# Ahead of a head loop: the rotary key is spread by GpSimd, two value tiles are evacuated by VectorE, and a chunk's rests are made later

## The chip, the cores and the metric

The kernel runs on 1 core of a Trainium2 chip. Times are microseconds on the device for one execution of the whole program. A core has TensorE (PE in the profile), VectorE (DVE), ScalarE (ACT), GpSimd (POOL) and SyncE (SP, which here only issues DMA transfers). Each works off its own list of instructions in order, and they wait for each other by semaphores.

## The reference, cut to what matters

Two blocks are computed on 256 tokens of width 1024 in float32. The change touches the second block, which puts 16 learned tokens ahead (so L = 272) and runs two kinds of causal attention side by side on the same normed input.

```python
u = rmsnorm_2(h, pre_norm_g[l])
proj = u @ w_in[l]
(cq, ckv, k_pe_raw, z_mla, fq, fk, fv, f_logit, z_fox, gate_a, gate_b) = jnp.split(proj, split_idx, axis=-1)
q = (rmsnorm_2(cq, mla_q_norm_g[l]) @ w_uq[l])      # 16 heads, 64 plain + 32 rotary columns
kv = (rmsnorm_2(ckv, mla_kv_norm_g[l]) @ w_ukv[l])  # 16 heads, 64 key + 64 value columns
k_pe = rope_2(k_pe_raw, pos)[:, None]               # one rotary key, the same for all heads
k_m = jnp.concatenate([k_nope, jnp.broadcast_to(k_pe, (B, MLA_HEADS, L, MLA_ROPE_DIM))], axis=-1)
o_mla = causal_block_attention(q_m, k_m, v_mla, MLA_SCALE)
o_fox = causal_block_attention(fox_heads(fq), fox_heads(fk), fox_heads(fv), FOX_SCALE, cum)
```

Here `k_m` is the keys of the latent attention (each head: its own 64 rows, and the rotary key that all share), `v_mla` its values, and `fq`, `fk`, `fv` belong to the attention with forget gates.

## The kernel before

Every float32 product is three matmuls of rounded halves, x_hi·w_hi + x_lo·w_hi + x_hi·w_lo (lines 472 to 474). So each operand must be split: ScalarE writes the rounded part (w_hi, s_hi, g_hi), and VectorE then writes the **rest**, value minus rounded part (w_lo, s_lo, g_lo). The large weights come in 56 chunks of 2 MB, each as two halves g = 0, 1 in `w_raw`. SyncE loads half g of chunk c once the rest of the same half of chunk c-1 is made (semaphore `w_lo_ok`). Small weights come in units (`w_side` into `s_raw`).

TensorE's order is written out by hand. Its results go to two accumulator banks `acc` in turn, as numbered by `acc_plan()`. Before tile n is begun, tile n-2 must have been evacuated (`acc_free`). Other results have banks of their own.

The stretch at issue lies ahead of the last loop, which runs over 32 heads (16 latent, 16 with forget gates). TensorE does there, in this order:

- `fk` 0 to 3: key tiles of the forget attention, from chunk `C_FK`. VectorE scales them (`keys_scaled`, line 2301). The tiles from `fk` 4 on need chunk `C_FK + 1`, in the loop.
- Transposes of the normed latents `cqn` in tiles 0, 1 and then 2 (`cqkv_turn`). ScalarE and VectorE split them into g_hi and g_lo. The transpose of tile 2 waits until the rest of tile 0 is made.
- `uk` 0 to 7: the latent keys, two heads each. ScalarE evacuates the even ones (1597, 1598), VectorE the odd ones (2335, 2336).
- `uv`: six value tiles of 512 columns, for the meta tokens (t = 2), then t = 0, then t = 1. Key `("uv", i, cc)` counts i in this order. ScalarE evacuates all six (`carry`, line 1240).
- `uq` 0 to 2: queries of heads 0 to 2. VectorE evacuates them (`query`, line 2361). They need the split unit `U_Q` (ScalarE 1226, then `rest_side` on VectorE, line 1743), and `uq` 2 goes into the bank of `uq` 0.
- Scores of heads 0 and 1 (line 1033), and the loop, which begins with the first half of what rides along with it: tile `fk` 4.

The shared rotary key stands in bank 6. ScalarE copies it into the keys `kT` of all 16 heads, four heads to an instruction (line 1587). `rest_half(c, slot, g)` makes half g of the rests of chunk c, 128x2048 (line 1830). GpSimd clears two tiles for the meta values (lines 450, 452), and issues eight small DMA transfers that place the meta rows `vu_rows` in them (line 458) once ScalarE has written these (`vu_ok`). VectorE waits for their landing (`um_landed`) in the loop, since `vu_rows` lies where `fk` 4 is to be written.

Of the kernel before, what the change touches and what calls it, by code (L numbers as in the profile page):

```python
# [23 lines left out]
ACT = mybir.ActivationFunctionType  # L24
AX = mybir.AxisListType.X

P = 128
R = 2
S = P * R
M = 16  # L30
L = M + S
D = 1024
KT = D // P
CH = 512
# [6 lines left out]
NH = 16  # L41
# [79 lines left out]
USE = acc_plan()  # L121
# [42 lines left out]
def two_blocks(nc, w_main, w_side, params, rows, c_l0, c_l1, c_b2, ident_d, x_d, x_t, meta_d, pos_d, out_d):  # L164
    ctx = ExitStack()
    with ctx:
# [3 lines left out]
        def sem(name):  # L170
            return ctx.enter_context(nc.semaphore(name))
# [27 lines left out]
        def ar(off, *shape):  # L199
            n = int(np.prod(shape))  # L200
            v = arena[:, off:off + n]
            names = "abcd"[:len(shape)]
            if len(shape) == 1:
                return v
            return v.rearrange(f"p ({' '.join(names)}) -> p {' '.join(names)}", **dict(zip(names[1:], shape[1:])))
# [46 lines left out]
        o_fox, y_mix = ar(7296, R, D), ar(9344, R, D)  # L252
        q_h, sm, pt = ar(14720, 2, S), ar(15232, 2, 416), ar(16064, 640)
        meta_p = [ar(off, R, GROUP * M) for off in (5760, 6016, 14720, 14976)]
        vu_rows, vf_rows = ar(1088, D)[0:M, :], [ar(4736, CH)[32 * c:32 * c + M, :] for c in range(2)]
        meta_v = [v_mm[:, 0:CH], v_mm[:, CH:D], f_vm[:, 0:CH], f_vm[:, CH:D]]
        root_p = stat[:, 8:24].rearrange("p (r a) -> p r a", r=R)
        b2c, b2k = ar(16704, L + S), ar(15232, L + P)
# [7 lines left out]
        hm, um, m_tmp = ar(11904, D), ar(12928, D), ar(3328, KT, M)  # L266
        sq = ar(9840, D)
        gain_u, scale_u, half_u, fin_u = pcol("norm_mix0", 0, KT), small[:, 32:34], small[:, 34:36], small[:, 36:38]
        kp, f_row = ar(2560, L), ar(2832, 4, L)
        last_gh, last_gl, last_sh, last_sl = x_hi[:, 2:4, M:L], x_lo[:, 2:4, M:L], x_hi[:, 4:8, M:L], x_lo[:, 4:8, M:L]  # L270
        o_mla = XN
        ffn_flat = ffn_nat[:, :, :, :].rearrange("p a r n -> p (a r n)")
# [34 lines left out]
        def landed(i):  # L307
# [15 lines left out]
        sc_ps, nm_ok, p_ok, pt_ps, pt_ok, ptm_ok, o_ps, o_ok = (  # L323
            sem(n) for n in ("sc_ps", "nm_ok", "p_ok", "pt_ps", "pt_ok", "ptm_ok", "o_ps", "o_ok"))
        k_ok, cum_ok = sem("k_ok"), sem("cum_ok")
        f_ps, f1_ok, f2_ok, ncum_ok, kpe_ps, kp_ok, kr_ps = (
            sem(n) for n in ("f_ps", "f1_ok", "f2_ok", "ncum_ok", "kpe_ps", "kp_ok", "kr_ps"))
        th_ok, z_ok, meta_part, xm_ok = sem("th_ok"), sem("z_ok"), sem("meta_part"), sem("xm_ok")
        vm_ok, uk_ps, uk_act, uk_dve = sem("vm_ok"), sem("uk_ps"), sem("uk_act"), sem("uk_dve")
        mp_ok, og_ps, og_ok, hx_ok, vu_ok = sem("mp_ok"), sem("og_ps"), sem("og_ok"), sem("hx_ok"), sem("vu_ok")  # L330
# [70 lines left out]
        def _(pool):  # L401
# [46 lines left out]

            pool.wait_ge(hg_ok, R)
            pool.memset(f_vm, 0.0).then_inc(blank_ok, 1)  # L450
            pool.wait_ge(tp_ready, ST["cqkv"] + ST_TILES["cqkv"])
            pool.memset(v_mm, 0.0).then_inc(blank_ok, 1)
            pool.wait_ge(blank_ok, 2)
# [15 lines left out]
        def _(pe):  # L469
# [665 lines left out]
            for n in range(3):  # L1135
                mla_query(n)
            pe.wait_ge(k_ok, 1)
            pe.wait_ge(uk_dve, 2)
            evacuated(("uk", 1), ("uk", 5))
            for n in range(2):  # L1140
# [73 lines left out]
        def _(act):  # L1214
# [368 lines left out]
            act.activation(stat[:, 31:32], stat[:, 31:32], ACT.Exp, scale=0.0)  # L1583
            split_main(C_FK + 1, (C_FK + 1) % 2)
            act.wait_ge(kr_ps, 1)
            for a in range(0, NH, 4):
                act.activation(kT[64:P, a:a + 4, :], bank[6][64:P, 0:L].rearrange("p (a l) -> p a l", a=1)
                               .to_broadcast([64, 4, L]), ACT.Copy)
            split_st("cqkv", x_tile(cst_h), lambda k: pcol("q_norm", k), ks=(0, 1))
            split_st("cqkv", x_tile(cst_h, 0), lambda k: pcol("q_norm", k), a=0, ks=(2,))  # L1590
            for p in range(0, 8, 2):
# [11 lines left out]
            act.drain().then_inc(k_ok, 1)  # L1603
            for i, t in enumerate((2, 0, 1)):
                for cc in range(2):
                    if (i, cc) == (1, 1):
                        act.drain().then_inc(vu_ok, 1)
                    if t == 2:
                        carry(vu_rows[:, cc * CH:(cc + 1) * CH], ("uv", i, cc), rows=M)
                    else:  # L1610
                        carry(v_m[:, t, cc * CH:(cc + 1) * CH], ("uv", i, cc))
                if i == 0:
                    act.wait_ge(uk_ps, 4)
                    split_side(U_Q)
            meta_pairs()
# [117 lines left out]
        def _(dve):  # L1733
# [7 lines left out]
            def rest_side(u):  # L1741
                dve.wait_ge(s_hi_ok, u + 1)
                dve.tensor_tensor(s_lo[:, u % 2, :], s_raw[:, u % 2, :], s_hi[:, u % 2, :], ALU.subtract).then_inc(s_lo_ok, 1)
# [84 lines left out]
            def rest_half(c, slot, g):  # L1828
                dve.wait_ge(w_hi_ok, 2 * c + g + 1)
                dve.tensor_tensor(w_lo[:, slot, 4 * g:4 * g + 4, :], w_raw[:, g, :, :],  # L1830
                                  w_hi[:, slot, 4 * g:4 * g + 4, :], ALU.subtract).then_inc(w_lo_ok, 1)
# [483 lines left out]
                dve.tensor_scalar(cqn[:, i, 256:384], cn[:, i, 256:384], root_col(3 + i), None, ALU.mult)  # L2315
            dve.tensor_scalar(cqn[0:M, 0, 256:384], cn[0:M, 0, 256:384], stat[0:M, 27:28], None, ALU.mult).then_inc(xn_ready, 1)
            keys_scaled(1)
            rest_half(C_FK + 1, (C_FK + 1) % 2, 0)
            keys_scaled(2)
            rest_st("cqkv", x_tile(cst_h), x_tile(cst_l), lambda k: pcol("q_norm", k), ks=(0, 1))  # L2320
            rest_st("cqkv", x_tile(cst_h, 0), x_tile(cst_l, 0), lambda k: pcol("q_norm", k), a=0, ks=(2,))
# [7 lines left out]
            for p in range(1, 8, 2):  # L2329
                if p % 4 < 2:  # L2330
                    b = acc_in(("uk", p))
                else:
                    dve.wait_ge(uk_ps, p // 4 * 2 + 2)
                    b = uk_bank[p % 4]
                dve.tensor_copy(kT[0:64, 2 * p, :], b[0:64, 0:L])
                ins = dve.tensor_copy(kT[0:64, 2 * p + 1, :], b[64:P, 0:L])
                ins.then_inc(acc_free[USE[("uk", p)] % 2] if p % 4 < 2 else uk_dve, 1)
            rest_side(U_Q)
            rest_half(C_FK + 1, (C_FK + 1) % 2, 1)

            def forget_sums():

# [100 lines left out]
            for n in range(2 * NH):  # L2443
                keys = RIDERS[n]
                if n in FOX_PAIRS:
                    head_masked(n + 1)
                if n + 3 < NH:
                    query(n + 3)
                if n == LOGS_AT + 2:
                    forget_sums()  # L2450
                if n + 3 == NH - 1:
                    gate_rows()
                take = {"fk": keys_scaled, "fq": queries_scaled}
                if n == 0:
                    dve.wait_ge(um_landed, 16 * GROUP)
                if len(keys) == 2:
                    take[keys[0][0]](keys[0][1])
                if n:
                    head_root(n - 1)
                dve.wait_ge(pt_ps, A2 + n + 1)  # L2460
                dve.tensor_copy(pt[:, 0:384], bank[5][:, 0:384]).then_inc(pt_ok, 1)
                if n + 2 < NH or n in FOX_PAIRS:
                    head_masked(n + 2)
                turned = ()
                if n in MLA_TURNS:
                    turned = [("o_mla", k) for k in MLA_TURNS[n]]
                if n in FOX_TURNS:
                    turned = [("o_fox", k) for k in FOX_TURNS[n]]
                for name, k in turned:
                    rest_st(name, lambda k: y_hi[:, k, :], lambda k: y_lo[:, k, :], ks=(k,))  # L2470
                for c, g in HALVES.get(n - 1, ()):
                    if (c, g) != (C_FV, 1):
                        rest_half(c, c % 2, g)
                if n and n % GROUP == 0:
                    group_out(n // GROUP - 1)
                if len(keys) == 2:
                    take[keys[1][0]](keys[1][1])
                elif keys:
                    gate(keys[-1])
                    after_key(keys[-1])  # L2480
                if (C_FV, 1) in HALVES.get(n, ()):
                    rest_half(C_FV, C_FV % 2, 1)
                if n in (1, 5):
                    rest_side(U_Q + 2 + n // 4)
# [193 lines left out]
```

## Time and profile before

| | us |
|---|---|
| median of 3 runs | 955.57 (955.03 to 956.99) |
| the profiled execution's own time | 956.61 |
| its span, from the first to the last instruction | 954.8 |
| TensorE busy | 930.5, or 97% |
| VectorE busy | 580.2, or 61% |
| ScalarE busy | 479.3, or 50% |
| GpSimd busy | 38.8, or 4% |

The span is what the trace shows. The profiled execution's own time is some 1.8 us longer than its span. Times of single rows are counted from the span's start. A matmul's end is modelled, and matmuls overlap, so that the distance from one start to the next says more than a duration.

### The profile page before, as it was taken

Reading aid. Unit: us, or ns where it says so; the run is one execution under the profiler, and the core shown is the slowest. Engines: PE = TensorE matmul, PEld = TensorE weight load, DVE = VectorE, ACT = ScalarE, POOL = GpSimd, SP = SyncE. Lnnn points to the kernel's source line nnn. Section 1 sums busy time; section 2 is a strip of 40 time slices with the busy share of each in tenths; the row PEclk is TensorE's granted clock in tenths of the full one; section 3 lists DMA queues with packets and bytes.
Section 4 is the critical chain, followed back from the end, with each engine's and each line's share of the span. In section 5 each row is a group of like instructions: output and inputs, shape, how many; then the busy total and the mean of one; then the engine's idle time right before and its main releaser. Section 6 shows DMA issues by size and latency. Waiting matters only on the chain.

```text
span 954.8 us, 13629 instructions
## 1 busy us (share of the span) xinstructions
PE 930.5 (97%) x5017; PEld 775.3 (81%) x5017; DVE 580.2 (61%) x1061; ACT 479.3 (50%) x773; POOL 38.8 (4%) x67
## 2 busy tenths in 40 slices
PE   6999999999999999999999999999999999999996
PEld 6877778888888899878888888889987878878775
DVE  5866857646355578567355453776665565565565
ACT  6565566344353547556353443686354445445442
POOL 1013200000000000000000000001011000000000
PEclk9999999999999999999999999999999999999998
DMA  8542256554635522236645546232433242433541
GB/s 304 213 177 89 93 190 220 196 201 147 238 142 213 184 89 90 89 131 242 223 152 199 196 153 238 94 134 80 189 101 127 100 161 89 177 132 132 174 158 44
DMA packets 26375, 150.43 MB, mean 158 GB/s; under 512 B 3664, under 2 KB 3920, under 8 KB 12112
## 3 DMA queue, kind: packets, MB, share of 16 engines
q1 hardware_dynamic: 24912, 147.44, 42.3%
q0 software_dynamic: 1408, 2.25, 0.8%
q8 instruction: 35, 0.57, 0.2%
q14 instruction: 20, 0.16, 0.1%
HBM read 148.50 MB, written 1.05 MB: 157 GB/s over the span
## 4 chain that ended last, share of the span: by engine, by line
PE 83%; DVE 8%; ACT 4%; DMA 2%; issue 2%; DVEq 1%; ACTq 0%; SPq 0%
PE bank L472 24%; PE bank L473 23%; PE bank L474 23%; DVE w_lo L1830 2%; DMA w_raw<-w_main_dram 2%; PE bank L543 1%; PE bank L1033 1%; PE bank L752 1%; DVE arena L2217 1%; PE bank L1048 1%; PE bank L1086 1%; PE bank L890 1%; PE bank L1068 1%; PE bank L1069 1%; PE bank L866 1%
## 5 line engine op out<-in xcount | busy, mean ns | idle before, releaser
L472 PE MATMUL bank<-w_hi,x_hi 128*128 128x512 f32 (+2 forms) x640 | 259.7, 406 | 1.3 <-DVE w_lo L1738 0.8
L473 PE MATMUL bank<-w_lo,x_hi 128*128 128x512 f32 (+2 forms) x640 | 249.9, 390 | 0.0
L474 PE MATMUL bank<-w_hi,x_lo 128*128 128x512 f32 (+2 forms) x640 | 249.5, 390 | 0.0
L1738 DVE TENSOR_TENSOR w_lo<-w_raw,w_hi 128x2048 fp32r<-128x2048 f32 x50 | 114.5, 2292 | 75.3 <-ACT w_hi L1219 74.3
L472 PEld LDWEIGHTS bank<-w_hi,x_hi 128*128 128x128 f32 x640 | 120.6, 188 | 30.0 <-issue 4.1
L474 PEld LDWEIGHTS bank<-w_hi,x_lo 128*128 128x128 f32 x640 | 120.2, 188 | 27.4
L1219 ACT ACTIVATE w_hi<-w_raw 128x2048 fp32r<-128x2048 f32 x54 | 103.4, 1918 | 76.9 <-DMA w_raw<-w_main_dram 70.9
L473 PEld LDWEIGHTS bank<-w_lo,x_hi 128*128 128x128 f32 x640 | 120.6, 188 | 22.3
L1830 DVE TENSOR_TENSOR w_lo<-w_raw,w_hi 128x2048 fp32r<-128x2048 f32 x51 | 116.2, 2284 | 5.0 <-ACT w_hi L1280 4.8
L1280 ACT ACTIVATE w_hi<-w_raw 128x2048 fp32r<-128x2048 f32 x50 | 94.8, 1906 | 14.6 <-DMA w_raw<-w_main_dram 14.1
L472 PE MATMUL bank<-x_hi,w_hi 128*128 128x256 f32 (+1 forms) x272 | 80.4, 296 | 9.0 <-DVE w_lo L1840 8.4
L1428 ACT ACTIVATE ffn_nat<-bank,stat 128x256 f32<-128x256 f32 x44 | 20.9, 474 | 132.3 <-PE bank L474 132.3
L473 PE MATMUL bank<-x_lo,w_hi 128*128 128x256 f32 (+1 forms) x272 | 77.8, 286 | 0.0
L474 PE MATMUL bank<-x_hi,w_lo 128*128 128x256 f32 (+1 forms) x272 | 77.8, 286 | 0.0
L2090 DVE SCALAR_TENSOR_TENSOR ffn_nat<-bank,stat,ffn_nat 128x256 f32<-128x256 f32 x44 | 21.1, 480 | 86.6 <-ACT ffn_nat L1428 86.6
L1507 ACT ACTIVATE arena<-arena,small 128x144 f32<-128x144 f32 x64 | 29.5, 461 | 75.8 <-DVE small L2194 75.8
L472 PE MATMUL bank<-s_hi,g_hi 128*128 128x512 f32 x166 | 65.4, 394 | 0.4 <-ACT arena L1240 0.4
L474 PE MATMUL bank<-s_hi,g_lo 128*128 128x512 f32 x166 | 65.5, 395 | 0.0
L473 PE MATMUL bank<-s_lo,g_hi 128*128 128x512 f32 x166 | 65.3, 393 | 0.0
L472 PEld LDWEIGHTS bank<-x_hi,w_hi 128*128 128x128 f32 x272 | 52.5, 193 | 11.5 <-issue 9.7
L472 PE MATMUL bank<-w_hi,s_hi 128*128 128x512 f32 x128 | 53.2, 415 | 0.7 <-DVE h L2021 0.3
L473 PEld LDWEIGHTS bank<-x_lo,w_hi 128*128 128x128 f32 x272 | 52.5, 193 | 0.0
(372 smaller groups left out, 1460.4 us busy)
## 6 DMA issues: line engine op xcount, KB each, us to landing
w_raw<-w_main_dram SPq DMA_DIRECT2D x111, 1024.0 KB, 4.9
s_raw<-w_side_dram SPq DMA_DIRECT2D x51, 512.0 KB, 4.2
w_raw<-w_main_dram SPq DMA_DIRECT2D x2, 512.0 KB, 6.5
h<-x_dram SPq DMA_DIRECT2D x2, 512.0 KB, 10.7
arena<-rows_dram POOLq DMA_DIRECT2D x2, 512.0 KB, 4.1
arena<-x_t_dram SPq DMA_DIRECT2D x1, 768.0 KB, 7.0
out_dram<-arena SPq DMA_DIRECT2D x1, 512.0 KB, 2.6
out_dram<-arena SPq DMA_DIRECT2D x2, 256.0 KB, 2.1
```

The source lines that it names most:

```text
L472: pe.matmul(out, ah, bh, start=first, stop=False)
L473: pe.matmul(out, ah, bl, start=False, stop=False)
L474: return pe.matmul(out, al, bh, start=False, stop=last)
L543: ins = pe.transpose(b[:, M + r * P:M + (r + 1) * P], src(r, k), ident[:, :])
L752: ins = pe.transpose(bank[2][:, ks * S + r * P:ks * S + (r + 1) * P], ffn_nat[:, 1, r, ks * P:(ks + 1) * P], ident[:, :])
L1219: act.activation(w_hi[:, slot, 4 * g:4 * g + 4, :], w_raw[:, g, :, :], ACT.Copy).then_inc(w_hi_ok, 1)
L1280: act.activation(w_hi[:, slot, 4 * g:4 * g + 4, :], w_raw[:, g, :, :], ACT.Copy).then_inc(w_hi_ok, 1)
L1428: act.activation(ffn_nat[:, 0, r, :], acc[(n0 + r) % 2][:, 0:256], ACT.Silu, scale=stat[:, 24 + r:25 + r]).then_inc(silu_ok, 1)
L1507: ins = act.activation(tiles(r), tiles(r), ACT.Exp, bias=small[:, s0 + 2 + r:s0 + 3 + r], accum_out=small[:, s0 + 4 + r:s0 + 5 + r])
L1738: dve.tensor_tensor(w_lo[:, slot, 4 * g:4 * g + 4, :], w_raw[:, g, :, :], w_hi[:, slot, 4 * g:4 * g + 4, :], ALU.subtract).then_inc(w_lo_o ...
L1830: dve.tensor_tensor(w_lo[:, slot, 4 * g:4 * g + 4, :], w_raw[:, g, :, :], w_hi[:, slot, 4 * g:4 * g + 4, :], ALU.subtract).then_inc(w_lo_o ...
L2090: dve.scalar_tensor_tensor(out=ffn_nat[:, 1, r, :], in0=acc[b_][:, 256:512], scalar=root_col(r), in1=ffn_nat[:, 0, r, :], op0=ALU.mult, op ...
```

## The change

Five things are edited.

1. ScalarE copies the rotary key once, 64x272, from bank 6 to SBUF (`kr_row`), and GpSimd writes it from there into the 16 heads, in four instructions, ahead of clearing `v_mm`. TensorE waits for the last of them (`kt_ok`) ahead of the first scores.
2. The two value tiles of t = 0, `("uv", 1, 0)` and `("uv", 1, 1)`, are evacuated by VectorE and no longer by ScalarE.
3. `rest_half` of chunk `C_FK + 1`, half 0, moves on VectorE from ahead of `keys_scaled(2)` to behind `rest_side(U_Q)`, where half 1 is.
4. `vu_rows` moves to other addresses, and VectorE's wait on `um_landed` from n = 0 to n = 2 of the loop.
5. ScalarE signals `vu_ok` ahead of its split of `U_Q`.

```diff
-        vu_rows, vf_rows = ar(1088, D)[0:M, :], [ar(4736, CH)[32 * c:32 * c + M, :] for c in range(2)]
+        vu_rows, vf_rows = ar(2880, D)[32:32 + M, :], [ar(4736, CH)[32 * c:32 * c + M, :] for c in range(2)]
...
-        kp, f_row = ar(2560, L), ar(2832, 4, L)
+        kp, f_row, kr_row = ar(2560, L), ar(2832, 4, L), ar(2560, L)[64:P, :]
...
             pool.memset(f_vm, 0.0).then_inc(blank_ok, 1)
+            pool.wait_ge(blank_ok, 1)
+            pool.wait_ge(kr_ok, 1)
+            for a in range(0, NH, 4):
+                ins = pool.tensor_copy(kT[64:P, a:a + 4, :], kr_row.rearrange("p (a l) -> p a l", a=1).to_broadcast([64, 4, L]))
+            ins.then_inc(kt_ok, 1)
+            pool.wait_ge(kt_ok, 1)
             pool.wait_ge(tp_ready, ST["cqkv"] + ST_TILES["cqkv"])
             pool.memset(v_mm, 0.0).then_inc(blank_ok, 1)
...
             pe.wait_ge(k_ok, 1)
+            pe.wait_ge(kt_ok, 1)
...
             act.wait_ge(kr_ps, 1)
-            for a in range(0, NH, 4):
-                act.activation(kT[64:P, a:a + 4, :], bank[6][64:P, 0:L].rearrange("p (a l) -> p a l", a=1)
-                               .to_broadcast([64, 4, L]), ACT.Copy)
+            act.activation(kr_row, bank[6][64:P, 0:L], ACT.Copy).then_inc(kr_ok, 1)
...
             for i, t in enumerate((2, 0, 1)):
                 for cc in range(2):
-                    if (i, cc) == (1, 1):
-                        act.drain().then_inc(vu_ok, 1)
                     if t == 2:
                         carry(vu_rows[:, cc * CH:(cc + 1) * CH], ("uv", i, cc), rows=M)
-                    else:
+                    elif t == 1:
                         carry(v_m[:, t, cc * CH:(cc + 1) * CH], ("uv", i, cc))
                 if i == 0:
+                    act.drain().then_inc(vu_ok, 1)
                     act.wait_ge(uk_ps, 4)
                     split_side(U_Q)
...
             keys_scaled(1)
-            rest_half(C_FK + 1, (C_FK + 1) % 2, 0)
             keys_scaled(2)
...
+            for cc in range(2):
+                key = ("uv", 1, cc)
+                dve.tensor_copy(v_m[:, 0, cc * CH:(cc + 1) * CH], acc_in(key)[:, :]).then_inc(acc_free[USE[key] % 2], 1)
             rest_side(U_Q)
-            rest_half(C_FK + 1, (C_FK + 1) % 2, 1)
+            for g in range(2):
+                rest_half(C_FK + 1, (C_FK + 1) % 2, g)
...
-                if n == 0:
+                if n == 2:
                     dve.wait_ge(um_landed, 16 * GROUP)
```

VectorE, before: the last copies of `uk` (2335, 2336), the rest of `U_Q` (1743), one rest of the chunk (1830), and the queries of heads 0 to 2 (2361).

```order
L2335 COPY arena<-bank 64x272 [waits uk_ps]
L2336 COPY arena<-bank 64x272
L1743 TENSOR_TENSOR s_lo<-s_raw,s_hi 128x1024 [waits s_hi_ok]
L1830 TENSOR_TENSOR w_lo<-w_raw,w_hi 128x2048 [waits w_hi_ok]
L2361 TENSOR_TENSOR arena<-bank,arena 128x256 [waits acc_ready0]
L2361 TENSOR_TENSOR arena<-bank,arena 128x256 [waits acc_ready1]
L2361 TENSOR_TENSOR arena<-bank,arena 128x256 [waits sc_ps,acc_ready0]
```

VectorE, after the change, at the same place (the queries have line 2368 there).

```order
L2338 COPY arena<-bank 64x272 [waits uk_ps]
L2339 COPY arena<-bank 64x272
L2343 COPY arena<-bank 128x512 [waits acc_ready0]
L2343 COPY arena<-bank 128x512 [waits acc_ready1]
L1747 TENSOR_TENSOR s_lo<-s_raw,s_hi 128x1024 [waits s_hi_ok]
L1834 TENSOR_TENSOR w_lo<-w_raw,w_hi 128x2048 [waits w_hi_ok] x2
L2368 TENSOR_TENSOR arena<-bank,arena 128x256 [waits acc_ready0]
L2368 TENSOR_TENSOR arena<-bank,arena 128x256 [waits acc_ready1]
L2368 TENSOR_TENSOR arena<-bank,arena 128x256 [waits sc_ps,acc_ready0]
```

Two copies of value tiles have come in ahead of the rest of `U_Q`, and two rests of the chunk now stand ahead of the first query, where one stood.

GpSimd, after the change, from the first clearing (450) on: the four copies of the rotary key (454), the second clearing (458) and the eight transfers of the meta rows (464).

```order
L450 MEMSET arena 128x1024 [waits hg_ok]
L454 COPY arena<-arena 64x1088 [waits kr_ok,blank_ok]
L454 COPY arena<-arena 64x1088 x3
L458 MEMSET arena 128x1024 [waits tp_ready,kt_ok]
L464 DMA arena<-arena 16x2x64 [waits vu_ok,blank_ok]
L464 DMA arena<-arena 16x2x64 x7
```

The second clearing and all transfers behind it now stand behind the copies.

## Rows read from the trace of the kernel before

**Rows 1.** The page's head: its span.

```profile
span 954.8 us, 13629 instructions
```

**Rows 2.** Stretches: length, busy us (instructions) of PE, PEld, DVE, ACT, POOL; PEclk, DMA share, GB/s.

```profile
8.41:14.09 5.68, 5.68 (x26) 5.68 (x27) 3.99 (x8) 3.77 (x9) 0.00 (x0) 1.00 1.02 418
14.20:19.90 5.70, 5.70 (x50) 5.70 (x49) 3.65 (x8) 5.58 (x11) 0.00 (x0) 1.00 0.75 305
632.00:649.12 17.12, 16.18 (x102) 13.24 (x100) 11.28 (x21) 11.73 (x25) 4.99 (x9) 1.00 0.27 87
649.12:947.00 297.88, 296.69 (x1680) 248.17 (x1678) 181.30 (x377) 140.28 (x268) 8.27 (x17) 1.00 0.36 128
```

**Rows 3.** Timeline of PE: start, duration, what [idle before <-releaser].

```profile
633.83 0.29 PE L474 MATMUL bank<-x_hi,w_lo 128*128 128x272 f32 x1
634.37 0.20 PE L541 MATMUL bank<-ident,arena 16*128 16x16 f32 x1 [0.25 <-DVE g_lo L1763]
...
642.10 0.39 PE L474 MATMUL bank<-s_hi,g_lo 128*128 128x512 f32 x1
...
642.82 0.40 PE L474 MATMUL bank<-s_hi,g_lo 128*128 128x512 f32 x1
643.66 0.50 PE L472 MATMUL bank<-s_hi,g_hi 128*128 128x512 f32 x1 [0.45 <-ACT arena L1240]
...
646.74 0.28 PE L474 MATMUL bank<-g_hi,s_lo 128*128 128x256 f32 x1
647.11 0.39 PE L472 MATMUL bank<-g_hi,s_hi 128*128 128x256 f32 x1
```

**Rows 4.** Timeline of DVE.

```profile
107.80 0.52 DVE L1783 TENSOR_SCALAR stat<-stat 128x4 int32<-128x4 int32 x1
...
629.91 2.27 DVE L1830 TENSOR_TENSOR w_lo<-w_raw,w_hi 128x2048 fp32r<-128x2048 f32 x1
632.20 0.44 DVE L2301 TENSOR_TENSOR arena<-bank,ffn_nat 128x272 f32<-128x272 f32 x1
633.74 0.88 DVE L1763 SCALAR_TENSOR_TENSOR g_lo<-bank,par,g_hi 128x256 fp32r<-128x256 f32 x2 [1.09 <-ACT g_hi L1256]
...
637.02 0.43 DVE L2328 SCALAR_TENSOR_TENSOR arena<-arena 16x272 f32<-16x272 f32 x1
...
640.87 0.44 DVE L2336 COPY arena<-bank 64x272 f32<-64x272 f32 x1
643.17 1.23 DVE L1743 TENSOR_TENSOR s_lo<-s_raw,s_hi 128x1024 fp32r<-128x1024 f32 x1 [1.86 <-ACT s_hi L1226]
644.31 2.28 DVE L1830 TENSOR_TENSOR w_lo<-w_raw,w_hi 128x2048 fp32r<-128x2048 f32 x1
646.62 0.85 DVE L2361 TENSOR_TENSOR arena<-bank,arena 128x256 f32<-128x256 f32 x2
...
680.50 4.49 DVE L1830 TENSOR_TENSOR w_lo<-w_raw,w_hi 128x2048 fp32r<-128x2048 f32 x2
```

**Rows 5.** DVE's copy-like instruction of 128x512 from a bank, all of that line.

```profile
L1855 DVE SCALAR_TENSOR_TENSOR arena<-bank,arena x4: 679/680/682, 31.2 to 40.7; 128x512 f32<-128x512 f32 x4
```

**Rows 6.** Timeline of ACT.

```profile
629.24 3.97 ACT L1587 ACTIVATE arena<-bank 64x1088 f32<-64x1088 f32 x4
633.23 0.84 ACT L1256 ACTIVATE g_hi<-bank,par 128x256 fp32r<-128x256 f32 x2
...
657.28 3.70 ACT L1280 ACTIVATE w_hi<-w_raw 128x2048 fp32r<-128x2048 f32 x2
```

**Rows 7.** Timeline of POOL.

```profile
106.80 1.50 POOL L436 TENSOR_SCALAR arena<-arena 128x512 f32<-128x512 f32 x1
...
635.00 0.95 POOL L452 MEMSET arena<- 128x1024 f32 x1 [21.17 <-PE bank L543]
644.33 4.03 POOL L458 DMA_DIRECT2D arena<-arena  x8 [8.38 <-ACTq L1607]
```

**Rows 8.** Transfers issued from 630 to 660 us: issuer, count, KB each, us to landing.

```profile
w_raw<-w_main_dram SPq DMA_DIRECT2D x2, 1024.0 KB, 4.7
```

More of the change, by code:

```diff
@@ L325, in two_blocks @@
         k_ok, cum_ok = sem("k_ok"), sem("cum_ok")
-        f_ps, f1_ok, f2_ok, ncum_ok, kpe_ps, kp_ok, kr_ps = (
-            sem(n) for n in ("f_ps", "f1_ok", "f2_ok", "ncum_ok", "kpe_ps", "kp_ok", "kr_ps"))
+        f_ps, f1_ok, f2_ok, ncum_ok, kpe_ps, kp_ok, kr_ps, kr_ok, kt_ok = (
+            sem(n) for n in ("f_ps", "f1_ok", "f2_ok", "ncum_ok", "kpe_ps", "kp_ok", "kr_ps", "kr_ok", "kt_ok"))
         th_ok, z_ok, meta_part, xm_ok = sem("th_ok"), sem("z_ok"), sem("meta_part"), sem("xm_ok")
```

## Prediction

> **What bounds the kernel now.** I read the page first: a span of 954.8 us [rows 1], of which TensorE is busy 97%. Then the stretches. From the loop's first riding tile (649.12) to the last matmul (947.00) TensorE is busy for 296.69 of 297.88 us, so 1.19 us are idle in all [rows 2]. The edits lie in the 17.12 us ahead of that, where it is busy for 16.18. Modelled ends hide part of the waiting there, so I count by distances from start to start: three matmuls of 512 columns take 642.82 - 642.10 = 0.72 us, 0.24 each [rows 3], and 50 of 256 columns 5.70 us, 0.114 each [rows 2], which makes about 0.12 for 272. The stretch holds 18 of 512 (4.3 us), 18 of 256 (2.1), 48 of 272 (5.8), and 15 small ones (eight scores, seven transposes) at up to 0.15 (2.2): 14.4 us. Some 2.8 us are waits. TensorE is the bound on both sides of the change, and its order is fixed: what it loses or gains in these 17 us it keeps.
>
> The timelines say who ends each wait. The transpose of latent tile 2 could have followed at 633.96 and starts at 634.37, released by VectorE [rows 3]. VectorE was late because ScalarE was: its g_hi pieces begin at 633.23, right behind four copies of the rotary key, 3.97 us from 629.24 [rows 4, 6]. The fifth `uv` tile starts at 643.66, on ScalarE's evacuation of the third. `uq` 2 starts at 647.11, some 0.25 us late, on VectorE's query(0) of 646.62 [rows 3, 4].
>
> **The change part by part.** Clock times are those of before; one shift is subtracted at the end.
>
> Rotary key. ScalarE's four copies (0.99 each) become one of a quarter of the columns, between 0.4 and 1.0 us, so it is free by about 630. keys_scaled(2) starts at 632.20, when `fk` 2 is done, and the first transposes follow directly on TensorE. Near 632.4 g_hi of tile 0 can then begin, and its rest is written by about 633.4, since VectorE's keys_scaled(2) is over at 632.20 + 0.44 [rows 4]. TensorE's last matmul ahead of it starts at 633.83, and 0.13 behind that it could go on [rows 3]. So the wait of 634.37 - 633.96 = 0.41 us goes: **-0.4**, and all behind it moves up by as much. What is late next is the VectorE chain below. Edit 3 frees VectorE at 629.91 to 632.18, but keys_scaled(2) waited for its matmuls anyway (it starts at 632.20): nothing there.
>
> GpSimd's copies. No row shows this operation. Bounds from the nearest rows: clearing 1024 columns, 0.95 us, gives 1.01 for 1088; a TENSOR_SCALAR of 512 columns, 1.50 us, gives 3.19 [rows 7]. Four of them from 629.7 on end between 633.8 and 642.5. The first scores want them behind `uq` 2, after 647.8 (647.11 and six matmuls): hidden by 5 us at the worst. I take a value near the low end, some 1.5 each, since a plain copy is nearer to the clearing in work. Even at 642.5 the second clearing ends at 643.5 and the eight transfers are issued (4.03 us [rows 7]) by about 647.5. VectorE now wants them at n = 2, after 657: nothing.
> The Trainium skill ("GPSIMD Engine Reference", section Engine selection) says that one-input operations run at roughly line rate, by estimate 0.9 us a copy and 3.6 in all. The TENSOR_SCALAR row (one tensor input, 2.9 ns a column) does not agree for its operation; neither value changes the sum.
>
> Value tiles. The third `uv` tile's last matmul starts at 642.10 and lasts 0.39, so VectorE, idle since 641.3 [rows 4], copies it from 642.5; a 512-column instruction from a bank takes 0.68 [rows 5]. The fourth (642.82 + 0.40) is copied 643.25 to 643.9. TensorE's fifth tile starts near 643.3 and no longer at 643.66. That 0.4 is no gain in the end, since the next wait is set elsewhere.
>
> The VectorE chain ahead of query(0). Before: rest of `U_Q` at 643.17 (held by ScalarE's s_hi), one chunk rest at 644.31, query(0) at 646.62 [rows 4]. Now the rest of `U_Q` starts behind the second copy, 643.9, and its successor 1.14 later (643.17 to 644.31 in the row), 645.04. Two chunk rests in a row last 4.49, and the next starts about 0.09 before the end of the last, 4.40 [rows 4]. So query(0) starts at 645.04 + 4.40 = 649.44, which is 2.82 us later. Queued behind it are queries 1 and 2 and the masking of head 0. TensorE waits for it at once: `uq` 2 takes the bank of `uq` 0, and follows 0.49 us behind query(0), 649.93 for 647.11 [rows 3]. `uq` 0 and 1 still run near 645.3 to 646.7, so there is nothing to do in between. Bounds of this term: with the copies free (2 x 0.68 less, held then by ScalarE's s_hi as before) it is one rest, 2.2; with each copy at 1.0 it is 3.4. I take **+2.8**.
>
> Edits 4 and 5. `vu_ok` comes some 1.5 us earlier and the wait for the landings later. The transfers were issued from 644.33 to 648.36 [rows 7], well ahead of the loop's first turn, so VectorE had no wait there to lose. Nothing.
>
> Loads. SyncE's load of half 0 of the next chunk goes out at about 647, and no longer at 632, half 1 at about 649. Each megabyte takes 4.7 us to land [rows 8], and one behind the other with the 0.5 MB side unit they end by about 656. ScalarE wants them at 657.28 [rows 6], which itself moves 2.4 us later: hidden, by 3 us or so. If that cover went, a microsecond would delay the split of a chunk that TensorE wants only three riding turns later (`fq` 0): still nothing at first.
>
> **Sum.** -0.4 + 2.8 = +2.4 us. The profiled execution took 956.61, of which the span is 954.8; it would be 959.0 with a span of 957.2. It lies 1.04 above the median of the three runs. On that median: 955.57 + 2.4 = **958.0 us**, +0.25%. A measurement of this kernel can tell about 0.2%, 1.9 us, from no change.
>
> **The rivals.**
>
> *Relief of ScalarE outweighs (faster).* The evacuations by two engines remove waits of TensorE between `uk` and the scores. Its price is bounded by the stretch: all 2.8 us gone, 952.8. It decides only if query(0) starts before 646.62 + 0.41 - 1.9 = 645.1. Behind the two copies and the rest of `U_Q` VectorE is at 645.04 with no chunk rest made, so both would have to cost nothing. For it: the waits are there. Against it: VectorE is in order. 4%.
>
> *Made up later (same).* TensorE's shift is taken back by waits in the loop that stood for other reasons. They hold 1.19 us in all [rows 2], so +1.2, 956.8. Against it: those found are releases by VectorE, which shifts along. 12%.
>
> *The clock falls.* TensorE is without work from about 647.0 (646.74 + 0.28 [rows 3]) to 649.9. The rows of the start show what a low clock costs: in 5.68 us from 8.41 on, after an idle start, it did 26 matmuls, in the 5.70 us from 14.20 on 50 [rows 2]. The granted clock column reads 1.00 in both, but the pace is half, as of 1.2 and 2.4 GHz. If the wait brings this back for as long, 5.7 x (1 - 26/50) = 2.7 us are added: 960.7. Against it: it needs the wait to be long enough, which no row tells. 12%.
> The Trainium skill ("TensorE: Matmul & The Clock Gate", Part 1) says that the default is the throttled state and that activity releases it; the start agrees, and a gap of 3 us is not shown by any run yet.
>
> *GpSimd holds up VectorE.* At 107.80 a VectorE instruction on 128x4 took 0.52 us and ended with GpSimd's at 106.80 + 1.50 = 108.30 [rows 4, 7]. If the copies are still running at 636.6, L2328 (row at 637.02, both inputs in SBUF) waits for one to end, and the `uk` copies and all of the chain with it. It needs copies of more than (636.6 - 629.7) / 4 = 1.7 us; the wait is then 1.1 to 2.7, say 1.7: 959.7. 15%.
> By the Trainium skill ("SBUF — State Buffer", Who interferes with whom) this port pair is an exclusive lock that two-input VectorE instructions and reading GpSimd ones take whole; the row at 107.80 agrees.
>
> **How the numbers follow.** The sum as it stands has 57%, the four rivals 4, 12, 12 and 15. Of the 57, some 14 lie below +1.9 us, given the bounds of 2.2 and 3.4 of its large term and the spread of the medians. Slower by over 0.2%: 43 + 12 + 15 = 70%. Within: 14 + 12 = 26%. Faster: 4%. The range reaches from the lower end of "made up later", 956.5, to 960.4, just short of the clock case: it leaves out 4 + some 4 + some 8%.
>
> **What would show it.** Right: TensorE waits some 3 us for VectorE's query ahead of the third `uq`, near 646.5; ahead of it on VectorE two 128x2048 rests without a gap; the transpose of latent tile 2 without a wait; the first riding tile 2.4 us later than before. Wrong: query(0) less than 1.5 us later; a wait of TensorE on GpSimd; PE idle behind 652 that shrank by more than 0.5 us; matmuls of 0.21 us distance behind the wait; L2328 longer than 0.5 us.

## The result and the profile after

The changed kernel takes 959.83 us, the median of 8 executions (957.76 to 960.19), against 955.66 for the kernel before (8 executions, 954.87 to 956.99). The ratio is 1.0034, with a 95% interval of 1.0025 to 1.0043: slower, by 2.4 to 4.1 us. (The two medians alone lie 4.2 us apart, a ratio of 1.0044: they rest on the larger of the two groups that follow.) The eight times do not lie evenly. Three are 957.76, 958.02 and 958.58, and five lie between 959.78 and 960.19.

The profiled execution (959.88) is one of the five. Its page begins:

```profile
span 958.1 us, 13632 instructions
```

The waits of TensorE behind 648 us show one that was not there before, the first of these two; the second stood there before as well, with line 1086 and the same 0.3 us:

```profile
PE bank L478 <- DVE arena L2368: 3.0, 1, 3.0
PE bank L1092 <- ACT arena L1678: 0.3, 1, 0.3
```

L2368 is query(n) of the changed kernel. TensorE's timeline around it, and where the latent tile 2 is transposed (L547), for [rows 3]:

```profile
631.31 0.60 PE L549 MATMUL bank<-ident,arena 128*128 128x128 f32 x4
...
633.35 0.23 PE L547 MATMUL bank<-ident,arena 16*128 16x16 f32 x1
...
642.29 0.50 PE L478 MATMUL bank<-s_hi,g_hi 128*128 128x512 f32 x1
...
645.59 0.28 PE L480 MATMUL bank<-g_hi,s_lo 128*128 128x256 f32 x1
648.87 0.39 PE L478 MATMUL bank<-g_hi,s_hi 128*128 128x256 f32 x1 [3.00 <-DVE arena L2368]
...
649.67 2.62 PE L1039 MATMUL bank<-arena 128*128 128x144 f32 x8
...
652.54 0.43 PE L480 MATMUL bank<-x_hi,w_lo 128*128 128x272 f32 x1
652.77 0.43 PE L478 MATMUL bank<-x_hi,w_hi 128*128 128x272 f32 x1
...
654.34 0.29 PE L479 MATMUL bank<-x_lo,w_hi 128*128 128x272 f32 x1
654.47 0.28 PE L480 MATMUL bank<-x_hi,w_lo 128*128 128x272 f32 x1
```

The transpose has lost its wait. The third query tile starts behind a wait of 3.00 us. The first matmuls of the riding tile then follow each other at 0.23 us, and later ones at 0.13. VectorE's timeline, for [rows 4]:

```profile
631.51 0.44 DVE L2305 TENSOR_TENSOR arena<-bank,ffn_nat 128x272 f32<-128x272 f32 x1 [2.21 <-PE bank L480]
...
636.03 0.43 DVE L2331 SCALAR_TENSOR_TENSOR arena<-arena 16x272 f32<-16x272 f32 x1
...
641.55 1.39 DVE L2343 COPY arena<-bank 128x512 f32<-128x512 f32 x2 [1.24 <-PE bank L480]
642.86 1.21 DVE L1747 TENSOR_TENSOR s_lo<-s_raw,s_hi 128x1024 fp32r<-128x1024 f32 x1
643.99 4.48 DVE L1834 TENSOR_TENSOR w_lo<-w_raw,w_hi 128x2048 fp32r<-128x2048 f32 x2
648.40 0.74 DVE L2368 TENSOR_TENSOR arena<-bank,arena 128x256 f32<-128x256 f32 x2
```

Two copies, the rest of `U_Q`, two chunk rests and the queries follow one another without a gap. GpSimd, for [rows 7], writes the rotary key in 4.21 us, 1.05 a copy, and clears the second tile behind it:

```profile
629.10 4.21 POOL L454 COPY arena<-arena 64x1088 f32<-64x1088 f32 x4 [15.94 <-ACT arena L1593]
634.07 0.95 POOL L458 MEMSET arena<- 128x1024 f32 x1 [0.75 <-PE bank L549]
```

The clock is read from a view of stretches (columns as in [rows 2]). The stretch is from the third query tile's first matmul to head 2's scores, where both kernels issue the same matmuls. Before:

```profile
647.11:652.33 5.22, 5.22 (x38) 5.06 (x39) 3.73 (x10) 1.67 (x5) 1.25 (x3) 1.00 0.84 308
```

After, the same, and inside it the slow part:

```profile
648.87:655.73 6.86, 6.86 (x39) 6.38 (x39) 4.65 (x15) 1.39 (x6) 0.00 (x0) 0.75 0.79 322
649.80:653.30 3.50, 3.50 (x15) 3.02 (x14) 2.21 (x7) 1.00 (x4) 0.00 (x0) 0.53 0.99 401
```

The granted clock is 1.00 before and 0.75 after. In the 3.5 us from 649.80 on it is 0.53: nearly all of them at the lower of the two levels, 1.2 GHz. What TensorE did ahead of it is wait 3.00 us and run 1 us of matmuls. The stretch is 1.64 us longer.

The other seven executions have no profile, but each has the granted clock's mean over the whole kernel. The five near 960 read 0.996, 0.996, 0.995, 0.997 and 0.994, the three near 958 read 0.997, 0.997 and 0.999. Half speed for 3.5 of 958 us is 0.002 of that mean. So these figures fit a clock that fell in the five and not in the three, but a single one of them proves little: kernels with no long wait read 0.997 to 0.999 in nearly all executions, and now and then 0.995 or 0.996.

**Where the time went.** Starts in two executions can't be compared directly: the four transposes ahead of this stretch start at 631.31 after and at 632.00 before, for reasons further up, where TensorE's work was not changed (over all the profiles of this document they start between 630.78 and 632.37). So I count from them. Third query tile: 15.11 us behind them before, 17.56 after, +2.45. Head 2's scores: 20.33 and 24.42, +4.09, of which 1.64 is the clock. With the 0.69 taken off, that is 3.4, near the 3.3 us between the spans.

### The profile page after: what moved, and what is told of

It is laid out like the page before. It is cut to its first block, busy times and chain, and to the rows that moved or that the text cites. A ratio compares the mean times of both kernels' runs of the same rounds, so it can differ in the third digit from the quotient of the medians.

```text
span 958.1 us, 13632 instructions
## 1 busy us (share of the span) xinstructions
PE 930.7 (97%) x5017; PEld 775.3 (81%) x5017; DVE 581.8 (61%) x1063; ACT 474.7 (50%) x768; POOL 43.0 (4%) x71
## 3 DMA queue, kind: packets, MB, share of 16 engines
HBM read 148.50 MB, written 1.05 MB: 156 GB/s over the span
## 4 chain that ended last, share of the span: by engine, by line
PE 82%; DVE 8%; ACT 4%; DMA 3%; DVEq 1%; issue 1%; SPq 0%; ACTq 0%
PE bank L478 24%; PE bank L479 23%; PE bank L480 23%; DMA w_raw<-w_main_dram 3%; DVE w_lo L1834 2%; PE bank L549 1%; PE bank L1039 1%; PE bank L758 1%; DVE arena L2221 1%; PE bank L1054 1%; PE bank L1092 1%; PE bank L896 1%; PE bank L1075 1%; PE bank L1074 1%; PE bank L872 1%
```

## The experiments

Ten kernels were run, one of them twice. Each row of this table is one profiled execution, in us counted from the four transposes; the wait is TensorE's ahead of the third query tile.

| kernel | latent tile 2 | 5th value tile | 3rd query tile | the wait | from there to head 2's scores | head 2's scores |
|---|---|---|---|---|---|---|
| before | 2.37 | 11.66 | 15.11 | under 0.2 | 5.22 | 20.33 |
| changed | 2.04 | 10.98 | 17.56 | 3.0 | 6.86 | 24.42 |
| half 0 back | 2.04 | 10.98 | 15.37 | 0.8 | 5.25 | 20.62 |
| half 0 alone | 2.35 | 11.64 | 17.28 | 2.3 | 6.81 | 24.09 |
| filled wait | 2.04 | 10.99 | 17.57 | 0.5 | 5.23 | 22.80 |
| longer wait | 2.04 | 10.99 | 19.93 | 5.4 | 6.59 | 26.52 |
| key alone | 2.04 | 11.65 | 15.09 | under 0.2 | 5.23 | 20.32 |
| half 1 behind the queries | 2.04 | 10.98 | 14.39 | none | 5.22 | 19.61 |
| values alone | 2.40 | 11.31 | 15.70 | 0.8 | 5.23 | 20.93 |
| wait between | 2.04 | 10.98 | 16.67 | 2.1 | 5.25 | 21.92 |
| key and half 1 | 2.04 | 11.72 | 14.88 | none | 5.22 | 20.10 |
| the same with the value tiles | 2.05 | 10.98 | 14.40 | none | 5.21 | 19.61 |
| half 1 behind the queries, again | 2.04 | 10.99 | 14.40 | none | 5.22 | 19.62 |

**Half 0 back.** The changed kernel, with half 0's rest in its old place.

```diff
             keys_scaled(1)
+            rest_half(C_FK + 1, (C_FK + 1) % 2, 0)
             keys_scaled(2)
...
             rest_side(U_Q)
-            for g in range(2):
-                rest_half(C_FK + 1, (C_FK + 1) % 2, g)
+            rest_half(C_FK + 1, (C_FK + 1) % 2, 1)
```

> The changed kernel with half 0 of the chunk's rests back in its old place, ahead of keys_scaled(2); one rest stands ahead of query(0). Theory (the second rest on the way to query(0) is the delay, the low clock behind the wait the remainder): one rest less, 2.2 us, so the wait ahead of the third query tile shrinks from 3.0 us to under 1, the clock stays up, and the time is before +0.2 us (-0.4 for the latent transposes, +0.6 for the value copies on VectorE): 955.9, with no execution near 960. Rival A (GpSimd's copies or the value copies on VectorE are what costs): still +2 or more, 957.6 to 959. Rival B (the loads of the next chunk, which go out later, cost the remainder beyond +2.4): about +0.2 too, but then the next experiment but one (fillers) stays near 959.5.

956.29 us (11 executions, 955.53 to 957.78) against 956.19 for before on that chip, ratio 1.0001 [0.9992, 1.0010]. The waits of TensorE behind 630:

```profile
PE bank L478 <- DVE arena L2368: 0.8, 1, 0.8
```

The loss is gone with this one rest (head 2's scores come at 20.62, for 24.42 and 20.33 before), and the low clock with it: the stretch takes 5.25 us. Rival A falls. GpSimd shows what the rest does in its old place, beside the copies:

```profile
628.67 6.36 POOL L454 COPY arena<-arena 64x1088 f32<-64x1088 f32 x4 [16.06 <-ACT arena L1593]
```

VectorE's rest in the same microseconds:

```profile
628.68 2.27 DVE L1834 TENSOR_TENSOR w_lo<-w_raw,w_hi 128x2048 fp32r<-128x2048 f32 x1
```

The four copies take 6.36 us and not 4.21. The 2.15 us more are about the length of the rest, 2.27, which began in the same moment and lost nothing. One by one, the first copy took 3.23 us and the other three about 1.1 each, as in the changed kernel all four do (1.09 to 1.11). So the first copy was held for as long as the rest ran. The Trainium skill ("SBUF — State Buffer", Who interferes with whom) calls the ports that the two engines share an exclusive lock, for which a VectorE instruction with two SBUF inputs contends with a GpSimd one that reads SBUF; the trace agrees. Nobody waits for these copies here, as they end at 635.0 and the first scores start at 647.0.

**Half 0 alone.** The kernel before, with only half 0's rest moved behind `rest_side(U_Q)`.

```diff
             keys_scaled(1)
-            rest_half(C_FK + 1, (C_FK + 1) % 2, 0)
             keys_scaled(2)
...
             rest_side(U_Q)
-            rest_half(C_FK + 1, (C_FK + 1) % 2, 1)
+            for g in range(2):
+                rest_half(C_FK + 1, (C_FK + 1) % 2, g)
```

> The kernel before with only half 0 of the chunk's rests moved behind the rest of U_Q; rotary key and value tiles as before. Theory: query(0) comes 2.1 us later than before (648.7 for 646.6), TensorE waits some 2.3 us ahead of the third query tile, +2.1 us: 957.7. If the clock falls behind a wait of that length too, another 1.7: 959.4 in some executions; I expect that it does not, or seldom. Rival A: without GpSimd's copies and the value copies nothing is lost, 955.6.

959.92 us (6 executions: 958.12, 959.01, 959.88, 959.95, 960.72, 960.80), ratio 1.0034 [1.0022, 1.0047]. The first two read a mean clock of 0.997 and 0.998, the other four 0.995 or 0.996. TensorE:

```profile
648.89 0.58 PE L472 MATMUL bank<-g_hi,s_hi 128*128 128x256 f32 x1 [2.31 <-DVE arena L2361]
```

The wait is the 2.3 us expected and the third query tile comes 2.17 us later. But I had expected the clock to stay up behind it, and it fell at once: the stretch to head 2's scores takes 6.81 us, and the clock view says

```profile
648.89:655.70 6.81, 6.81 (x39) 6.50 (x40) 3.87 (x11) 1.01 (x4) 0.00 (x0) 0.75 0.80 328
```

This one moved rest makes, alone, nearly all of the change's loss: +3.76 of +4.09 us at head 2's scores, and the same ratio.

**Filled wait.** The changed kernel with 20 matmuls, whose result nothing uses, in the wait.

```diff
             for n in range(3):
+                if n == 2:
+                    pe.wait_ge(k_ok, 1)
+                    for i in range(20):
+                        pe.matmul(bank[5][:, 0:L], x_hi[:, i % KT, 0:P], x_hi[:, (i + 1) % KT, :], start=True, stop=True)
                 mla_query(n)
```

> The changed kernel with 20 more matmuls of 128x272 on TensorE ahead of the third query tile (they read x_hi and write a free bank; nothing uses them), some 2.5 of the 3.0 us of the wait. Theory (the clock falls in most executions because of the wait, which costs 1.7 us each time): the wait keeps its length, the clock stays at its higher level, the first riding tile has matmuls at a distance of 0.126 us, and every execution is near before +2.4: 958.0, none at 960. Rival B (the remainder beyond +2.4 comes from loads or from GpSimd): two groups of times at 958 and 960 as in the changed kernel.

958.54 us (8 executions, 957.90 to 959.33), ratio 1.0024 [1.0014, 1.0035], that is +2.3 us. TensorE:

```profile
645.96 2.67 PE L1145 MATMUL bank<-x_hi 128*128 128x272 f32 x20
649.12 0.38 PE L478 MATMUL bank<-g_hi,s_hi 128*128 128x256 f32 x1 [0.49 <-DVE arena L2372]
```

and the stretch behind it:

```profile
649.12:654.35 5.23, 5.23 (x39) 5.07 (x39) 3.65 (x10) 1.02 (x4) 0.00 (x0) 1.00 1.00 407
```

The third query tile comes as late as in the changed kernel (17.57 us), since VectorE is as late, but the clock is 1.00 and the stretch takes 5.23. The group around 960 is gone: all eight lie within 1.5 us and read a mean clock of 0.997 or 0.998. So the fall of the clock comes from TensorE's idleness, and rival B (loads) falls: DMA is busier in this stretch (share 1.00) than in the changed kernel's (0.79). With 2.7 us of useless work added, head 2's scores come 1.6 us earlier than in the changed kernel. By the times the kernel lies 1.0024 over before, for 1.0034; the two intervals overlap, so that the size of the gain rests on the profiles.

**Longer wait.** A third rest instruction ahead of query(0).

```diff
             rest_side(U_Q)
+            dve.wait_ge(w_hi_ok, 2 * (C_FK + 1) + 1)
+            dve.tensor_tensor(w_lo[:, (C_FK + 1) % 2, 0:4, :], w_raw[:, 0, :, :],
+                              w_hi[:, (C_FK + 1) % 2, 0:4, :], ALU.subtract)
+            dve.drain()
             for g in range(2):
```

> The changed kernel with a third rest instruction of 128x2048 on VectorE ahead of query(0), which writes what the next one writes again. Theory: the wait ahead of the third query tile grows by 2.3 us to 5.3, and the clock falls behind it in every execution: before + 2.4 + 2.3 + 1.7 = 962.0, with no lower group. Rival C (the low clock comes by chance and has nothing to do with the wait's length): two groups, 960.3 and 962.

963.47 us (5 executions, 962.83 to 964.02), ratio 1.0075 [1.0061, 1.0089]. The wait is 5.37 us, the stretch behind it 6.59 at a granted clock of 0.78:

```profile
652.00 0.58 PE L478 MATMUL bank<-g_hi,s_hi 128*128 128x256 f32 x1 [5.37 <-DVE arena L2372]
```

Some 0.5 us of the wait itself was already at the low clock (its mean over the 5.37 us is 0.95), so that less of the slow time is left behind the wait. All five lie together, with no group 1.5 us lower, as expected of a wait that brings the clock down every time. Five are few, though: the changed kernel's 5 of 8 would give that by chance in one case of ten. The profiled one is the fastest of the five and its stage accounts for +6.2 us; the median is 1.0 higher than the 962.0 + 0.5 that were to be expected on this chip. The other four read a mean clock of 0.994, where the profiled one reads 0.997, so they spent longer at the low clock. Where, no profile shows; that stays open.

**Key alone.** The changed kernel with both rests and all value tiles as before.

```diff
-                    elif t == 1:
+                    else:
                         carry(v_m[:, t, cc * CH:(cc + 1) * CH], ("uv", i, cc))
...
             keys_scaled(1)
+            rest_half(C_FK + 1, (C_FK + 1) % 2, 0)
             keys_scaled(2)
...
-            for cc in range(2):
-                key = ("uv", 1, cc)
-                dve.tensor_copy(v_m[:, 0, cc * CH:(cc + 1) * CH], acc_in(key)[:, :]).then_inc(acc_free[USE[key] % 2], 1)
             rest_side(U_Q)
-            for g in range(2):
-                rest_half(C_FK + 1, (C_FK + 1) % 2, g)
+            rest_half(C_FK + 1, (C_FK + 1) % 2, 1)
```

> The kernel before with only the rotary key's part of the change: ScalarE copies it once, GpSimd spreads it; value tiles and both rests as before. Theory: the transpose of latent tile 2 loses its wait, -0.4 us, and nothing else moves: 0.05% under before, not to be told from no change, but in the profile the transpose goes at once. Half 0's rest runs on VectorE beside GpSimd's first copies, so these take some 2 us longer in sum than in the changed kernel. Rival A (GpSimd's copies delay VectorE or TensorE): +0.5 us or more.

956.59 us (11 executions) against 956.33, ratio 1.0001 [0.9992, 1.0010]. The transpose goes at once, as expected (2.04 for 2.37), and the copies take 6.49 us beside the rest. But the gain does not arrive: the third query tile stands where it stood (15.09 for 15.11). The fifth value tile waits longer for ScalarE, 0.74 us for the 0.45 of [rows 3]. ScalarE's timeline shows why:

```profile
640.68 1.29 ACT L1247 ACTIVATE arena<-bank 16x512 f32<-16x512 f32 x2 [0.43 <-PE bank L480]
642.14 1.06 ACT L1233 ACTIVATE s_hi<-s_raw 128x1024 fp32r<-128x1024 f32 x1 [0.17 <-issue]
643.10 1.07 ACT L1247 ACTIVATE arena<-bank 128x512 f32<-128x512 f32 x2
```

Before, the same three:

```profile
640.90 1.29 ACT L1240 ACTIVATE arena<-bank 16x512 f32<-16x512 f32 x2 [0.42 <-PE bank L474]
642.10 1.04 ACT L1226 ACTIVATE s_hi<-s_raw 128x1024 fp32r<-128x1024 f32 x1
643.04 1.28 ACT L1240 ACTIVATE arena<-bank 128x512 f32<-128x512 f32 x2
```

From the first value tile to the third it is 2.42 us instead of 2.14. The drain for `vu_ok`, which edit 5 puts ahead of the split, costs 0.26 us: the split starts 1.46 us behind the first value tile, and before it was 1.20. Before, it stood one tile further on, where TensorE no longer waited.

**Half 1 behind the queries.** The changed kernel with half 0 back, and half 1 behind query(1).

```diff
             keys_scaled(1)
+            rest_half(C_FK + 1, (C_FK + 1) % 2, 0)
             keys_scaled(2)
...
             rest_side(U_Q)
-            for g in range(2):
-                rest_half(C_FK + 1, (C_FK + 1) % 2, g)
...
             query(0)
             query(1)
+            rest_half(C_FK + 1, (C_FK + 1) % 2, 1)
```

> The changed kernel with half 0 of the rests back in its old place and half 1 behind query(1): no chunk rest stands ahead of query(0). Theory: the third query tile loses its wait; -0.4 us for the transposes and another -0.3 to -0.5 behind the value tiles: 0.8 us under before, 0.1%, on the edge of what can be told; no low clock. Rival D (half 1 then comes too late for the second half of the first riding tile, or delays query(2) and the masks): a new wait of up to 0.7 us, and the time of before.

955.26 us (11 executions, 954.44 to 956.16) against 956.33, ratio 0.9991 [0.9982, 0.9999]. VectorE now waits for TensorE at the queries, and the rest falls into its free time:

```profile
642.57 1.22 DVE L1747 TENSOR_TENSOR s_lo<-s_raw,s_hi 128x1024 fp32r<-128x1024 f32 x1
644.91 0.42 DVE L2367 TENSOR_TENSOR arena<-bank,arena 128x256 f32<-128x256 f32 x1 [1.13 <-PE bank L480]
645.61 0.42 DVE L2367 TENSOR_TENSOR arena<-bank,arena 128x256 f32<-128x256 f32 x1 [0.28 <-PE bank L480]
645.95 2.28 DVE L1834 TENSOR_TENSOR w_lo<-w_raw,w_hi 128x2048 fp32r<-128x2048 f32 x1
```

Rival D, a rest that comes too late for the riding tile, is not seen: head 2's scores come 0.72 us earlier than before.

**Values alone.** The kernel before with the two value tiles on VectorE.

```diff
-                    else:
+                    elif t == 1:
                         carry(v_m[:, t, cc * CH:(cc + 1) * CH], ("uv", i, cc))
...
+            for cc in range(2):
+                key = ("uv", 1, cc)
+                dve.tensor_copy(v_m[:, 0, cc * CH:(cc + 1) * CH], acc_in(key)[:, :]).then_inc(acc_free[USE[key] % 2], 1)
             rest_side(U_Q)
```

> The kernel before with only the two value tiles evacuated by VectorE; rests and rotary key as before. Theory: the rest of U_Q starts 0.7 us later (behind the second copy and no longer on ScalarE's s_hi), and query(0) with it; the fifth value tile starts 0.4 earlier, which gives nothing. TensorE's wait ahead of the third query tile grows to some 0.9 us, +0.6 us, 0.06%: same within what can be measured, no low clock. Rival E (relief of ScalarE outweighs): -0.4 or below.

956.92 us (11 executions) against 956.33, ratio 1.0009 [1.0000, 1.0018]. The wait and the shift are as expected, 0.8 and +0.6 us:

```profile
646.94 0.39 PE L472 MATMUL bank<-g_hi,s_hi 128*128 128x256 f32 x1 [0.80 <-DVE arena L2364]
```

**Wait between.** The kernel of "Half 0 back", with a rest of 128x1024 more ahead of half 1's.

```diff
             rest_side(U_Q)
+            dve.wait_ge(w_hi_ok, 2 * (C_FK + 1) + 2)
+            dve.tensor_tensor(w_lo[:, (C_FK + 1) % 2, 4:6, :], w_raw[:, 1, 0:2, :],
+                              w_hi[:, (C_FK + 1) % 2, 4:6, :], ALU.subtract)
+            dve.drain()
             rest_half(C_FK + 1, (C_FK + 1) % 2, 1)
```

> The changed kernel with half 0 back in its old place, and a rest of half the size (128x1024, written again by the next one) ahead of half 1: a wait ahead of the third query tile between the 0.8 us that left the clock up and the 2.3 us that brought it down. Theory: wait 2.0 us, before +1.5 us where the clock stays up, +3.1 where it falls; I expect both groups to occur. If all executions lie at +1.5, a wait of 2.0 us is short enough here.

958.90 us, ratio 1.0025 [1.0013, 1.0037]; the eight are 956.21, 956.91, 958.04, 958.46, 959.34, 959.85, 960.25, 960.39. The profiled one (958.46) waited 2.10 us and kept its clock:

```profile
649.04:654.29 5.25, 5.25 (x38) 5.09 (x39) 3.65 (x10) 1.02 (x4) 0.00 (x0) 1.00 0.75 276
```

Its stage accounts for +1.6 us. The four times above 959 fit a clock that fell. They were not profiled, but their mean clocks are 0.995 or 0.996, and those of the four below 959 are 0.997 or 0.998.

**Key and half 1, and the same with the value tiles.** Both have half 1 behind query(1) and signal `vu_ok` behind the split of `U_Q` (only that edit is shown). In the first all value tiles stay on ScalarE, in the second two are VectorE's.

```diff
                 if i == 0:
-                    act.drain().then_inc(vu_ok, 1)
                     act.wait_ge(uk_ps, 4)
                     split_side(U_Q)
+                    act.drain().then_inc(vu_ok, 1)
```

> The kernel before with the rotary key on GpSimd and half 1 of the rests behind query(1); all value tiles on ScalarE, vu_ok signalled behind the split of U_Q. Theory: -0.4 us at the latent transposes, -0.3 ahead of the third query tile (its wait for query(0)); the split of U_Q starts right behind the second value tile (1.20 us behind the first one's start, where with the drain ahead of it 1.46 were seen), so that nothing is lost at the fifth value tile: -0.7 us, 0.07% under before. Rival (the value copies on VectorE are what gives the last experiment but two its gain): -0.4 or less.

> The changed kernel with half 0 in its old place, half 1 behind query(1), and vu_ok signalled behind the split of U_Q (as in the best version so far but for the signal). Theory: VectorE reaches the rest of U_Q only behind the second value copy, later than ScalarE's split ends either way, so the earlier split gives nothing: the time of the best version so far, 0.9 us under before.

The first: 955.96 us against 956.04, ratio 0.9997 [0.9988, 1.0006]. The expectation missed. The split starts earlier, 1.31 us behind the first value tile (not the 1.20 expected), but the drain now holds the third value tile instead, which TensorE's fifth waits for (11.72 us for 11.66). With that, the 0.33 us won at the transposes is gone. The 0.23 us that the scores gain come from behind it: with no chunk rest ahead of query(0), the third query tile follows the fifth value tile by 3.16 us, for 3.45 before. The rival had named a gain of 0.4 or less, and it holds. The second: 955.40, ratio 0.9995 [0.9986, 1.0004]; its scores come at 19.61, as with the signal ahead of the split. That is as expected, since with the copies on VectorE nobody waits for ScalarE there. The two kernels differ only in the value tiles, so VectorE's copies are worth 0.49 us at the scores (19.61 for 20.10) once no rest stands ahead of the queries. The times alone, with overlapping intervals, do not separate the two.

**The best once more**, on the same chip.

> The best version so far once more, on the chip of the two above, to compare with them: 0.9 us under before, 0.1%.

955.43 us against 956.04, ratio 0.9993 [0.9984, 1.0002]. One of its two intervals lies just below 1 and the other reaches over it. The gain by the medians is 0.6 to 1.1 us, on the edge of what this kernel's times can tell. The profile gives 0.7.

## Why the prediction was right or wrong

**Right: the large term.** Put at +2.8 from the chain value copies, rest of `U_Q`, two chunk rests, query(0). Counted from the transposes, query(0) comes 2.47 us later with the 0.4 already taken off, where 2.8 - 0.4 = 2.4 was said. Experiments that undo (half 0 back) and isolate it (half 0 alone) give it back and bring it: 2.19 and 2.17 us for the rest. The value copies cost 0.6, as in the chain.

**Right: the gain at the latent transpose**, put at 0.4 and measured at 0.33. It is worth this only because the value tiles moved to VectorE. With the key alone the drain of edit 5 eats it. "Edits 4 and 5: Nothing" holds for the change as made, but hides a price of 0.15 to 0.26 us that ScalarE pays.

**Wrong: the sum as the likeliest case.** 958.0 is where three of the eight executions lie (mean 958.1). The median is 959.83, since in the others, by the one profile and the mean clocks, the clock falls. The step that failed is the weight of "The clock falls": 12%. It was the usual case, with 5 of 8 times above 959.7, and the filled wait shows the idle TensorE to be its cause. I had said of it that no row shows a wait of this length, and had then taken the absence of a row for a small chance. Its price was put at 2.7 us, from the start of the kernel, where the slow pace lasted 5.7 us. Here it lasted some 3.5 and cost 1.64. That the median lies in the range, 956.5 to 960.4, is luck. The range was drawn to end just short of the clock case, at 960.7 by that price, and so to leave out what then happened in most executions. It held because the price was 1.1 us too high: 958.0 + 1.64 is 959.6.

**Right: hidden parts.** GpSimd's copies took 1.05 us each, close to the lower bound of 1.01, and were over at 633.3, so VectorE's two-input instruction at 636.03 took its usual 0.43 us: the rival "GpSimd holds up VectorE" did not occur, and my 1.5 was too high. The row at 107.80, which I took to agree with the lock on two-input instructions, is a TENSOR_SCALAR with one tensor input, and does not bear on those; the copy of 3.23 us in "Half 0 back" does. The Trainium skill's line rate ("GPSIMD Engine Reference", Engine selection) gives by estimate 0.9, close to this copy, while the TENSOR_SCALAR of [rows 7] stays three times slower per column. The later loads were hidden. (In the opening sum 17.12 - 14.4 is 2.7 and not 2.8; it only bounds a rival.)

**Not seen:** "Made up later". In the changed kernel TensorE's other waits behind 648 are those of before. "Relief of ScalarE outweighs" was right in its place and wrong in this order of VectorE. The fifth value tile did start earlier, by 0.35 us more than the transposes give, and VectorE's queue took it back. With no rest ahead of the queries the same copies gain 0.49 us, in the version that clearly beats the changed kernel and lies under the one before by about what the times can tell.

## What to carry to other kernels

Work with slack is best moved by asking what stands behind it in the engine's order. Half 0's rest was needed some 2.5 us later than query(0) (649.12 for 646.62 before), and yet stood ahead of it. A rest in a gap of 2.3 us costs nothing, and the same rest in front of an evacuation that TensorE waits for costs nearly all of its length (2.2 us). A wait of 2 to 3 us on TensorE can have a second price in the half-speed stretch behind it, here 1.6 us in most executions; if the wait can't be removed, useless matmuls in it kept the clock up here. And executions that fall into two groups by 1.6 us ask for the clock row of that stretch before anything else.

## What the runs showed of the hardware

- TensorE's clock fell behind waits of 2.31, 3.00 and 5.37 us in the profiled executions. It stayed up behind 2.10, 0.80 and, with 2.67 us of matmuls in the gap, 0.49. By the times and the mean clocks, 2.1 to 3.0 us do it in some executions and not in others, 5.4 in all five. At the low level the pace was 0.23 us for 272 columns and 0.21 for 256, about half, and the loss 1.4 to 1.6 us. The Trainium skill ("TensorE: Matmul & The Clock Gate", Part 1) says that activity releases the throttle; these rows agree: in the changed kernel, with TensorE at work all the time, the clock of 0.53 from 649.80 to 653.30 is followed by 1.00.
- GpSimd copied 1088 float32 columns in 1.05 us (four in 4.21; 0.97 ns a column), from a source repeated four times. A VectorE instruction with two SBUF inputs beside it held it up for about its whole length: 6.36 and 6.49 us for four copies in place of 4.21, with one copy of 3.23 us beside three of 1.1.
- A drain on ScalarE between two activations cost 0.15 to 0.26 us. Ahead of the split it is 0.26 against the kernel before (1.46 us from the first value tile to the split, for 1.20), but 0.15 against the kernel with the signal behind the split (1.46 for 1.31); the difference is not explained.
